# The second layer of a two-block transformer kernel: the end of its delta rule by token tile, and the order of row products, value tokens and gates in its projections

## The reference, cut to what matters

```python
def odd_mixer(a_lat, a_ctx, w_in, conv_w, a_log, dt_bias, o_norm, w_out, need_ctx):
    lq, lk, lv, lg, lla, lbe = odd_project(a_lat, w_in, conv_w, a_log, dt_bias)
    cq, ck, cv, cg, cla, cbe = odd_project(a_ctx, w_in, conv_w, a_log, dt_bias)
    ...
    o_l, (o_cf, o_cb) = bidir_scan(gdn_chunked, ...)
    o_lat = odd_merge(o_l, lg, o_norm, w_out)

def odd_merge(o, g, o_norm, w_out):
    o = rms_norm(o.transpose(0, 2, 1, 3), o_norm) * jax.nn.silu(g.reshape(B, L, GDN_HEADS, GDN_DV))
    return o.reshape(B, L, GDN_WIDTH) @ w_out
```

## Time and profile before

| what | value |
|---|---|
| time, median of 3 runs | 2262.78 us (2261.61 to 2264.59) |
| the profiled execution's own time | 2263.13 us |
| its span | 2261.3 us |
| mean granted TensorE clock | 0.937 |
| TensorE busy | 2054.6 us (91%) |
| vector engine busy | 1511.4 us (67%) |
| scalar engine busy | 900.1 us (40%) |
| GpSimd busy | 140.4 us (6%) |
| DMA | 323.94 MB, mean 143 GB/s |

### The profile page before, as it was taken

How to read it: one execution, slowest core, us unless ns; L and a number is a source line. 1 busy time by engine, 2 the same in 40 slices (tenths; PEclk the granted TensorE clock), 3 DMA queues, 4 the chain that set the end, 5 groups by cost and what they waited for, 6 DMA issues and landing times. The chain is left out here.

```text
span 2261.3 us, 40156 instructions
## 1 busy us (share of the span) xinstructions
PE 2054.6 (91%) x16866; PEld 1836.8 (81%) x16866; DVE 1511.4 (67%) x2325; ACT 900.1 (40%) x1333; POOL 140.4 (6%) x231
## 2 busy tenths in 40 slices
PE   5998987999999788799996999899899989988997
PEld 4786865888888576589896899788789979887997
DVE  6866466997766757665645677768677666956444
ACT  3445443222222422322224444455444445554443
POOL 0100000101000010200210000000000000000000
PEclk7999988999999888899998999899889998988999
DMA  8531032555452454100003577343347744323552
GB/s 330 202 123 64 2 112 76 195 177 203 175 196 93 162 196 167 57 3 3 3 3 128 182 277 276 143 149 112 131 157 277 276 145 150 118 95 108 185 185 93
DMA packets 59133, 323.94 MB, mean 143 GB/s; under 512 B 6384, under 2 KB 7536, under 8 KB 32624
## 3 DMA queue, kind: packets, MB, share of 16 engines
q1 hardware_dynamic: 33360, 228.97, 28.5%
q0 software_dynamic: 25344, 92.29, 11.4%
q10 hardware_dynamic: 288, 0.66, 0.1%
HBM read 320.84 MB, written 1.05 MB: 142 GB/s over the span
## 5 line engine op out<-in xcount | busy, mean ns | idle before, releaser
L370 DVE TENSOR_TENSOR w_low<-raw,w_high 128x1024 fp32r<-128x1024 f32 (+1 forms) x408 | 473.2, 1201 | 241.2 <-ACT w_high L362 240.9
L362 ACT ACTIVATE w_high<-raw 128x1024 fp32r<-128x1024 f32 (+1 forms) x408 | 402.2, 1035 | 388.4 <-PE banks L400 380.9
L541 DVE SCALAR_TENSOR_TENSOR mod_rows<-mod_rows,silu_condition 128x1024 f32<-128x1024 f32 x176 | 212.4, 1221 | 49.2 <-DMA mod_rows<-rows_dram 46.5
L398 PE MATMUL banks<-ffn_a_l,w_high 128*128 128x256 f32 x704 | 199.7, 284 | 1.9 <-DVE ffn_hidden L996 1.9
L400 PE MATMUL banks<-ffn_a_h,w_low 128*128 128x256 f32 x704 | 199.1, 283 | 0.0
L399 PE MATMUL banks<-ffn_a_h,w_high 128*128 128x256 f32 x704 | 199.1, 283 | 0.0
L398 PE MATMUL banks<-mlp_a_l,w_high 128*128 128x512 f32 (+1 forms) x512 | 176.8, 345 | 11.9 <-DVE mlp_a_l L683 7.7
L527 POOL DMA_DIRECT2D mod_rows<-rows_dram x176 | 93.2, 530 | 1399.6 <-DVE mod_rows L541 1182.2
L399 PE MATMUL banks<-mlp_a_h,w_high 128*128 128x512 f32 (+1 forms) x512 | 175.2, 342 | 0.0
L400 PE MATMUL banks<-mlp_a_h,w_low 128*128 128x512 f32 (+1 forms) x512 | 175.0, 342 | 0.0
L398 PE MATMUL banks<-mlp_hidden_l,w_high 128*128 128x512 f32 (+1 forms) x512 | 173.3, 338 | 1.3 <-DVE mlp_hidden_l L1004 1.3
(11 more groups left out here) (596 smaller groups left out, 4888.9 us busy)
## 6 DMA issues: line engine op xcount, KB each, us to landing
raw<-panels_dram SPq DMA_DIRECT2D x204, 1024.0 KB, 4.8
mod_rows<-rows_dram POOLq DMA_DIRECT2D x176, 512.0 KB, 5.1
mod_0a_rows<-rows_dram SPq DMA_DIRECT2D x8, 1024.0 KB, 20.0
x_features<-x_features_dram SPq DMA_DIRECT2D x1, 2048.0 KB, 11.2
constants<-small_dram SPq DMA_DIRECT2D x1, 1672.5 KB, 6.8
silu_condition<-conditions_dram SPq DMA_DIRECT2D x2, 512.0 KB, 12.4
out_dram<-x_features SPq DMA_DIRECT2D x4, 256.0 KB, 2.1
constants<-small_dram SPq DMA_DIRECT2D x1, 736.5 KB, 5.2
```

Source lines behind the costliest of these rows:

```text
L362: self.nc.scalar.activation(self.wh[:, m % 2, cols], self.raw[:, slot, cols], ACT.Copy).then_inc(self.w_high, 1)
L370: self.nc.vector.tensor_tensor(self.wl[:, m % 2, cols], self.raw[:, slot, cols], self.wh[:, m % 2, cols].bitcast(F32), ALU.subtract).then_ ...
L398: self.nc.tensor.matmul(out, sh(k), ml(k), start=(opens and k == 0), stop=False)
L541: nc.vector.scalar_tensor_tensor(row if v == nv - 1 else self.scratch[:], row, 1.0, self.cond[v][:], ALU.mult, ALU.mult, accum_out=mod[:, ...
```

## The change

1. `linear` gets an argument `behind`, called behind each block that is taken out. `beside_v` and `beside_qk` take one row product ahead of the two convolutions, and `behind` one more behind each. The number of rows is unchanged.
2. The values in token order are copied out of PSUM by the scalar engine (`values_out`) and no more by the vector engine.
3. `decay_sums` moves from the fourth panel of `odd_v` to the second of `odd_qk`, `decay_sums_out` to the third; the three exps move behind the norm of queries and keys, the betas to the second panel of `odd_v`, and `state_decays` ahead of the key copies.
4. In the rule's last step the gate's silu is computed in two halves between the copies `T` of n = 2 and 3 and those that follow.
5. The rule's end goes by token tile: each direction's output is added, multiplied by the gate, squared and summed apart. The first weight panel is split in two halves between the tiles' steps, as soon as all outputs are made; the second panel is split behind `odd_out_h`.
6. The two tiles' products with the norm alternate by head with the split of the result. `whole_split` and `mixer_out` go.

```diff
@@ -375,6 +375,13 @@
         while self.split_next[which] <= m:
             (self.split_act if which == "act" else self.split_dve)(eng, self.split_next[which])
             self.split_next[which] += 1
+
+    def split_half(self, act, h):
+
+        m = self.m
+        assert self.split_next["act"] == m
+        self.split_act(act, m, parts=(h,))
+        self.split_next["act"] += h
...
@@ -833,6 +841,8 @@
                     if who[q] == which:
                         eng.wait_ge(done, q + 1)
                         evac(q, which, eng, self.ps[:, banks[q % nb], :]).then_inc(out[which], 1)
+                        if behind is not None:
+                            behind(which, eng)
...
         nc.scalar.activation(tmp[:], tmp[:], ACT.Ln, bias=1.0).then_inc(ln_ready, 1)
+        nc.scalar.activation(beta[:], ab[:, :, 16:32], ACT.Sigmoid).then_inc(beta_ready, 1)
+        act.wait_ge(beta_ready, 1)
+        nc.scalar.activation(nbeta[:], beta[:], ACT.Copy, scale=-1.0).then_inc(gates, 1)
...
 
-    gate_steps = {("dve", 1): gate_inputs, ("act", 1): gate_logs, ("dve", 2): log_decays, ("pe", 3): decay_sums,
-                  ("dve", 3): decay_sums_out, ("act", 3): gate_exps}
+    gate_steps = {("dve", 1): gate_inputs, ("act", 1): gate_logs, ("dve", 2): log_decays}
...
     def beside_v(which, eng, p):
-        beside(which, eng, 3)
+        beside(which, eng, 1)
...
 
+    def values_out(act, p):
+        for q in (2 * p, 2 * p + 1):
+            act.wait_ge(v_turned, q + 1)
+            nc.scalar.activation(v_tok[:, :, q * P:(q + 1) * P], ps[:, 4 + q % 2, :].rearrange("p (i n) -> p i n", n=P),
+                                 ACT.Copy).then_inc(v_ready, 1)
+
     def beside_qk(which, eng, p):
-        beside(which, eng, 3)
+        beside(which, eng, 1)
+        if which == "act" and p:
+            values_out(eng, p)
         if which == "act":
             if p == 0:
                 silu_of(eng, v_info, (6, 7), v_act)
+                values_out(eng, p)
             else:
                 silu_of(eng, qk_info, (2 * p - 2, 2 * p - 1), qk_act)
                 square_of(eng, (2 * p - 2, 2 * p - 1))
-        if which == "dve" and p == 1:
-            state_decays(eng)
+        if which == "pe" and p == 1:
+            decay_sums(eng)
+        if which == "dve" and p == 2:
+            decay_sums_out(eng)
         for q in (2 * p, 2 * p + 1):
             if which == "pe":
                 eng.wait_ge(v_act, q + 1)
@@ -1877,15 +1873,13 @@
                     last = nc.tensor.transpose(ps[:, 4 + q % 2, i * P:(i + 1) * P], pre[:, q, i * P:(i + 1) * P],
                                                c("ident"))
                 last.then_inc(v_turned, 1)
-            if which == "dve":
-                eng.wait_ge(v_turned, q + 1)
-                nc.vector.tensor_copy(v_tok[:, :, q * P:(q + 1) * P],
-                                      ps[:, 4 + q % 2, :].rearrange("p (i n) -> p i n", n=P)).then_inc(v_ready, 1)
 
     pr.linear("odd_v", 4, 2, 8, pr.features(high, low, N, KD, tall_offset), conv_out(8),
-              [], engines=("dve",), prior=ab_info, info=v_info, beside=beside_v)
+              [], engines=("dve",), prior=ab_info, info=v_info, beside=beside_v,
+              behind=lambda which, eng: beside(which, eng, 1))
     pr.linear("odd_qk", 4, 2, 8, pr.features(high, low, N, KD, tall_offset), conv_out(0),
-              [], engines=("dve",), prior=v_info, info=qk_info, beside=beside_qk, carry=False)
...
         for b in range(4):
+            pe.wait_ge(g_out, 1)
             pe.wait_ge(q_squared, b + 1)
...
         nc.scalar.activation(qT[:], qT[:], ACT.Exp, scale=-0.5).then_inc(q_root, 1)
+        gate_exps(act)
...
             .then_inc(q_normed, 1)
+        state_decays(dve)
...
+        def gate_silu(h):
+            part = gate[:, 4 * h:4 * h + 4, :]
+            nc.scalar.activation(part, part, ACT.Silu).then_inc(gate_ready, 1)
+
...
                     w_copy(u - 1)
+                if u + 1 == STEPS and n in (2, 3):
+                    gate_silu(n - 2)
             if u + 1 < STEPS:
...
         new_values(STEPS - 1)
-        outputs_out(STEPS - 1)
-
-    lats = 4
+        for d in range(2):
+            outputs_out(STEPS - 1, (d,))
+            dve.wait_ge(gate_ready, 2)
+            dve.wait_ge(o_out, late(STEPS - 1, d))
+            part = by_tile(gate, tiles[d][STEPS - 1])
+            nc.vector.scalar_tensor_tensor(part, part, c("gdn_o"), by_tile(y, tiles[d][STEPS - 1]), ALU.mult,
+                                           ALU.mult).then_inc(gated, 1)
+
...
+    high, low = (pr.sb(f"odd_out_{name}", [P, H, TL], F32R, ctx=inner) for name in ("h", "l"))
+    sq_ready, summed, logs_out, r_ready, scaled, high_ready, split = (pr.sem(f"odd_norm_{x}") for x in (
+        "squares_ready", "summed", "logs", "rstd_ready", "scaled", "high_ready", "split_ready"))
+    order = [tiles[d][STEPS - 1] for d in range(2)]
+    both_heads = lambda i: ps[:, 2 * i:2 * i + 2, :].rearrange("p b (h n) -> p (b h) n", n=P)
+
+    @pr.block.scalar
...
+        def squares(d):
+            i = order[d]
+            act.wait_ge(o_out, late(STEPS - 1, d))
+            for h in range(2):
+                nc.scalar.activation(sq[:, i, 4 * h:4 * h + 4, :], y[:, 4 * h:4 * h + 4, i * P:(i + 1) * P],
+                                     ACT.Square).then_inc(sq_ready, 1)
+
+        def logs_of(d):
+            act.wait_ge(summed, 2 * d + 2)
+            nc.scalar.activation(r[:, order[d]], both_heads(order[d]), ACT.Ln, bias=c("eps"),
+                                 scale=1.0 / GDN_DV).then_inc(logs_out, 1)
+
+        squares(0)
+        act.wait_ge(o_done, 4)
+        pr.split_half(act, 0)
+        logs_of(0)
+        squares(1)
+        pr.split_half(act, 1)
+        logs_of(1)
+        for d in range(2):
+            act.wait_ge(logs_out, d + 1)
+            nc.scalar.activation(r[:, order[d]], r[:, order[d]], ACT.Exp, scale=-0.5).then_inc(r_ready, 1)
+        for k in range(H):
+            act.wait_ge(scaled, k + 2)
+            nc.scalar.activation(high[:, k, :], y[:, k, :], ACT.Copy).then_inc(high_ready, 1)
+
+    @pr.block.tensor
+    def _(pe):
+        for d in range(2):
+            for h in range(2):
+                pe.wait_ge(sq_ready, 2 * d + h + 1)
+                nc.tensor.matmul(ps[:, 2 * order[d] + h, :], c("ones"),
+                                 sq[:, order[d], 4 * h:4 * h + 4, :].rearrange("p h n -> p (h n)"),
+                                 start=True, stop=True).then_inc(summed, 1)
+
+    @pr.block.vector
+    def _(dve):
+        pr.split_upto("dve", dve, pr.m)
+        dve.wait_ge(r_ready, 1)
+        dve.wait_ge(gated, 2)
+        nc.vector.tensor_tensor(by_tile(y, order[0]), by_tile(gate, order[0]), r[:, order[0]],
+                                ALU.mult).then_inc(scaled, 1)
+        dve.wait_ge(r_ready, 2)
+        for step in range(H + 1):
+            if step < H:
+                cols = slice(order[1] * P, (order[1] + 1) * P)
+                nc.vector.tensor_tensor(y[:, step, cols], gate[:, step, cols], r[:, order[1], step, :],
+                                        ALU.mult).then_inc(scaled, 1)
+            k = step - 1
+            if k >= 0:
+                dve.wait_ge(high_ready, k + 1)
+                nc.vector.tensor_tensor(low[:, k, :], y[:, k, :], high[:, k, :].bitcast(F32),
+                                        ALU.subtract).then_inc(split, 1)
```

More of the change, by code:

```diff
@@ L359, in split_act @@
             act.wait_ge(sem, self.in_loop(lambda x: self.ends[x][1], m - 2, q))
-        for h in range(2):
+        for h in parts:
             cols = slice(h * width // 2, (h + 1) * width // 2)
@@ L2418, in odd_mixer @@
     t.close()
-    gate_ready, done = pr.sem("odd_gate_ready"), pr.sem("odd_gated")
-    with ExitStack() as t:
-        @pr.block.scalar
-        def _(act):
-            nc.scalar.activation(gate[:], gate[:], ACT.Silu).then_inc(gate_ready, 1)
-        def gated(dve, _):
-            dve.wait_ge(gate_ready, 1)
-            dve.wait_ge(o_out, lats)
-            ch.then(dve, nc.vector.scalar_tensor_tensor(gate[:], gate[:], c("gdn_o"), y[:], ALU.mult, ALU.mult))
-        r, _, r_ready = pr.rstd(t, "odd_norm", y[:], [(o_out, lats)], [[h] for h in range(H)],
-                                TL, GDN_DV, c("ones"), meanwhile=gated)
-        @pr.block.vector
-        def _(dve):
-            for w in r_ready:
-                dve.wait_ge(*w)
-            for h in range(H):
-                nc.vector.tensor_tensor(y[:, h, :], gate[:, h, :], r[:, h, :], ALU.mult).then_inc(done, 1)
@@ L2446, in rope_tables @@
+    return high, low, [(split, H)], inner
 def rope_tables(pr, pos_in, cos, sin):
@@ L3159, in layer1 @@
             scope = ExitStack()
-            y, ready = odd_mixer(pr, mod, scope, norm("norm1", 1), [(late_in, 16)], beside, activate)
-            ready = mixer_out("odd_out", y, ready, mod, 1, TL, scope)
```

(5 more changed lines are left out.)

54 lines of the change are left out of this document (15 added, 39 removed).

## The result

The changed kernel takes **2228.03 us** (median of 4 runs, 2223.83 to 2232.82) against 2263.03 us (2261.61 to 2264.59) for the kernel before, run beside it: a ratio of 0.9846, 95% interval 0.9824 to 0.9868. Forecast were 2232.0 us and a range of 2227 to 2245. The profiled execution took 2229.53 us, its span is 2227.8 us.

What follows compares the result with a forecast made beforehand. The vector engine's cycle, held by row waits, set the pace from the fourth value panel; behind the rule, one serial chain did. 23.5 + 1.0 - 0.3 + 6.9 = 31.1 us off 2263.13 gave 2232.0 us, range 2227 to 2245.

Steps and rivals of the forecast that it cites:

- Term 1: Value and key panels: rows apart, values by scalar engine, sums moved; TensorE reaches the queries' sums 23.5 us earlier.
- 1.0 us: Last convolution ahead of the rule: starts when TensorE is done, no longer behind rows and copies; 1.0 us gained.
- 0.3 us: Chain ahead of the rule: `state_decays` and three small exps put into it; 0.3 us lost.
- Term 2: Rule's last step: the gate's silu halves lie in the scalar engine's idle stretches; cost 0, gain 0.
- Term 3: Rule's end by token tile: `odd_out` starts at about 1204.2 instead of 1211.11, 6.9 us earlier, bounds 5 and 8.
- weighed rule: TensorE's panels: the skill's 215.7 ns per 512 columns, set aside for the trace's 0.234 us; it would give 2227.7 us.
- Rival A: Value and key panels: rows landing after 7.5 us still hold the vector engine; 2240.5 us, chance 0.14.
- B: Rule's end: only 3 us shorter, from more scalar pieces or a late second panel; 2236 us, chance 0.12.
- C: Value and key panels: gain returns as another wait, or rows never held TensorE; 2263 us, chance 0.03.
- D: Value and key panels: TensorE without pauses gets the lower clock for long; slower, 2278 us, chance 0.03.

Runs made afterwards that it cites:

- e1: Changed kernel with all three rows of a value or key panel together again, ahead of the panel's two blocks; 2251.15 us.
- e2: Kernel before with only the rows apart, one ahead of a panel and one behind each block; 2235.95 us.
- e7: Changed kernel with the gate's silu undivided behind the rule's last step, ahead of the first squares; 2230.93 us.
- e14: Changed kernel with the ab product turned: 32 weight columns stationary, 512 tokens streaming, four small transposes back to token order; 2219.03 us.
- e9: Changed kernel with the gate's rows behind its copies from the second panel on, and the ab product's two rows one behind each block; 2226.14 us.
- e15: Changed kernel with e14's turned product, e9's rows (gate's last row behind the split), the end reordered with an early logarithm and its four bytes; 2212.56 us.
- e16: Changed kernel with one more allocation of four bytes a partition, written and read by nothing; 2229.52 us.
- e3: Kernel before with points 1 to 3 of the change, its gate silu and end as before; 2237.36 us.

## Why the prediction was right

**Term 1** came out as put: 23.73 us for 23.5. Its mechanism is shown from both sides (e1, e2). What the working had wrong is the company: it credited "values by scalar engine, sums moved" along with the rows, and called the `log_a` wait gone because `decay_sums` moved. e2 leaves both where they were, and the waits go all the same. The queries' sums began at 905.68, forecast 905.5 to 906. The stretch's waits for rows are 5.5 us, forecast under 12. A slip in the sum is small: the six small matmuls stand there with 0.9 us, at a transpose's price they are 0.6, and they took 0.6 (868.73 to 869.34).

The **1.0 us** of the last convolution and the **0.3 us** for `state_decays` and exps: together -0.96 for -0.7. The last convolution starts at 905.88, 0.2 us behind the start of the queries' sums and so with its block, as forecast. The lost 0.3 can't be seen: e2, which has them at their old place, needs 16.75 us from the queries' sums to the row sums, as the changed kernel does.

**Term 2**, nothing: e7 agrees.

**Term 3**: 6.49 for 6.9, inside its bounds. The chain on the scalar engine was read right, piece by piece; its pieces of half length cost a little more than half (1.04 to 1.06 for 0.97, 1.11 for 1.0), and the second sums came 0.61 us late where 0.3 was allowed. The second panel came in time, with no pause of TensorE.

The three terms' stretches together are 31.18 us for 31.1. The profiled execution is 2.4 us shorter still, of which the rule has 2.08; they were in no term, and e14, with the changed kernel's rule, has one longer than both kernels'. The median of the result lies another 1.5 us lower, at 2228.03 on the very edge of the forecast of 2228 to 2236. So the stretches were known to the microsecond, and the total is only good to some 4 us; that it fell just inside is luck.

**The weighed rule.** With the 215.7 ns of the Trainium skill (TensorE: Matmul & The Clock Gate, Wait — 56ns, not 53.3ns?) the estimate would have been 2227.7, against 2228.03 measured. The trace bears neither the rule nor that agreement out: in `odd_qk` of the changed kernel the products still follow each other at 0.23 us (904.99, 905.22, 905.45), not 0.216, and the stretch took what the row gave. The quickest pace in any profile here is 0.226 to 0.227 us, 440 to 443 products in 100 us, in the four kernels with the four bytes.

**Rival A** is refuted by waits of 0.4 us in `odd_v` and `odd_qk`. It was nearer than that sounds: the slot of the row at 859.40 had come free at 852.62, so this row landed 6.8 us later, and its wait was 0.27; A had set 7.5. **B** is refuted by E; **C** by e2; **D** by a clock of 1.00 from 834 to 906.

## What to carry to other kernels

When several short jobs share few buffers that a transfer refills, count from a buffer's release to its next use: spread the jobs so that other work fills it, and do so first, since waits further down may only be echoes of the first. Undo one part at a time in both directions: two parts that each look responsible need not add. Look also at a product with few moving columns: here 96 products of 32 columns took 18.5 us and the clock fell during them, and turned round, so that the long side moves, 24 products took 5.5. That brought 9.2 us, where taking out the pause beside it brought nothing that could be told. And when an edit adds an allocation, run the allocation alone before crediting the rest.

## What the runs showed of the hardware

- TensorE's clock fell during 96 products of 32 columns although the engine had no pause within them (e9: from 1.00 to 0.50 at 791.3 us, back at 811.8; in the changed kernel at 796.5, ahead of the pause). With the product turned and no pause above 0.8 us it stayed at 1.00 (e15). Removing only the pause gained nothing that could be told.
- At a granted clock of 1.00 the same products run at two paces, and which one goes with four bytes of allocation: 234 and 227 ns for `mlp_a` with 512 columns, but 118 and 120 ns for `ffn_a` with 256, in ten profiles without and four with the bytes. By what way the bytes act isn't known.
- e16's times fall into two groups some 9 us apart for one program. The groups' cause wasn't found.
- The same 16 sums took 3.72 us in the kernel before and 5.41 in e2 and e3, at a granted clock of 1.00 and of 0.68, and the old end 18.57 and 20.25 us. A wait's price isn't fixed; whether the quicker head or chance set the clock there isn't shown.
